# Low halves of weight blocks moved from GpSimd to VectorE, a beginning by halves of two blocks, and the closing norm's subtraction shared with GpSimd

## The chip, the cores and the metric

The kernel runs on one core of one Trainium2 chip. Its engines are TensorE (PE, products), VectorE (DVE), ScalarE (ACT), GpSimd (POOL) and SyncE (SP, which here only issues transfers). Each runs its own list of instructions in a fixed order, and they wait for each other through semaphores. The metric is the device time of one execution in microseconds (us); lower is better, and the verdict compares medians of runs.

## What is computed

A sequence of 512 positions of width 1024 passes through a macaron of layers, each with norms around it and, from the second half on, scales and shifts that a conditioning vector gives:

```
x = x + 0.5 * norm(swiglu(norm(x), w_gu, w_down))      # f1: width 2816
x = x + norm(hybrid_mixer(norm(x)))                    # gated recurrence and windowed attention
x = x + 0.5 * norm(swiglu(norm(x), w_gu, w_down))      # f2
x = layer_norm(x); retention; feed-forward (f3); neighbourhood attention; feed-forward (f4)
x = layer_norm(x)                                      # the closing norm

def rms_norm(x, g):
    y = x * lax.rsqrt(jnp.mean(x * x, axis=-1, keepdims=True) + RMS_EPS)
    return y * g

def swiglu(x, w_gu, w_down):
    gate, up = jnp.split(x @ w_gu, 2, axis=-1)
    return (jax.nn.silu(gate) * up) @ w_down
```

Everything is in float32.

## The kernel before, in words

**Products.** The activations lie as 8 chunks of 128 features by 512 positions, features on the partitions. A float32 product is made of three products of halves: a number is split into a high half (rounded to a shorter format) and a low half (what is left), and `products` issues three matmuls at L2072 (high weight, low activation), L2073 (low weight, high activation) and L2074 (high by high). Matmuls have 512 columns, or 256 where the positions are taken in two passes s = 0 and s = 1, as at the beginning and in the down products.

**A weight block.** Weights come in blocks of 128x1024 (512 KB; 128x768 for some of the first down product). SP loads a block into one of three raw buffers (the ring d_ring0 to 2), ScalarE casts it to the high half (L2394), and VectorE (L2764) or GpSimd (L3445) subtracts to get the low half; then the raw buffer is free for the next load. Which of the two does it is decided when the program is planned: by turns, except that VectorE does all of them for the down products of the third and fourth feed-forward ("dn3", "dn4") and where other chains of work are open. The first two blocks are cast and subtracted in halves of 512 columns (L2386, L2755).

**A swiglu unit.** For each 128 hidden features: gate and up products on TensorE; VectorE multiplies the gate by the norm's root (L3039); ScalarE takes silu (L2505); GpSimd multiplies by the root and the silu (L3451, the gate); VectorE multiplies by the up product in PSUM (L3052); ScalarE casts the result to its high half (L2514); VectorE subtracts for the low half (L3058, into `t_hid`). The down product waits for that last step of the last unit.

**A norm's root.** ScalarE squares the chunks, VectorE adds them up (L2881) and makes the last sum at L2887; TensorE sums over the partitions (L2208); ScalarE takes the root (L2440), VectorE the reciprocal (L2940) and a diagonal (L2944); TensorE turns it into a row (L2216). The second pass of the first norm goes this way at 17 to 39 us.

**Order.** A planner simulates the engines with a table of costs (a cast so long, a load so long) and lists each engine's steps by their due times; the program then holds these fixed lists. Every step keeps its place whatever happens on the chip.

**The closing norm's end.** For the second pass (256 positions) the variance's root is made as above while VectorE takes the mean row from each of the 8 chunks (`lead_z`, L2934, which reads the row from PSUM); when the root's row stands in PSUM, VectorE multiplies (`ln_apply`, L2993), ScalarE adds the shift and SP stores.

Of the kernel before, what the change touches and what calls it, by code (L numbers as in the profile page):

```python
# [40 lines left out]
SPARED = ()  # L41
# [142 lines left out]
class Plan(dict):  # L184
# [24 lines left out]
    def note(self, name, out, a, k):  # L209
# [118 lines left out]
    def run(self, families):  # L328
# [8 lines left out]
        while events:  # L337
# [3 lines left out]
            for engine in self.ops:  # L341
                while free[engine] <= t:
# [18 lines left out]
                    if op.table is not None and op.table != table:  # L361
# [34 lines left out]
def schedule(known=()):  # L396
# [124 lines left out]
    def assign(slot, after):  # L521
# [71 lines left out]
    def one_by_one(specs, segs):  # L593

        held = [block(sp[0], sp[1]) for sp in specs]
        for si, (t0, n) in enumerate(segs):
            force_tokens(t0, n)
            groups = []
            for (_, _, nk, src, outs), j in zip(specs, held):
                ready(j)  # L600
                b = bank()
                groups.append(put("mm", w=j, slot=where[j], lo=low[j], base=0, nk=nk, src=src, t0=t0, n=n, bank=b, po=0,
                                  before=seat(b, outs[0][1], len(items))))
# [192 lines left out]
    def last_norm(j, ready):  # L796
# [27 lines left out]
        for c in range(DC):  # L824
# [832 lines left out]
    first_ffn("f1", 1, "gu1", "dn1", "ffn1_post_g", lambda j, s: ("d_x1" if s else f"d_x0{j // 4}", 0),  # L1657
# [40 lines left out]
    for it in items:  # L1698
        if it.kind in ("ada", "load") or it.kind == "prep" and not it.q:
# [14 lines left out]
        if it.kind == "prep_lo":  # L1714
            it.update(preps[it.j], kind="prep_lo")
# [253 lines left out]
def sync_program(e, w, S, m, dram, items, loads):  # L1969
# [33 lines left out]
    def serve(it):  # L2003
        if it.kind == "setup":
            x_all, x_in = m.X[:, :].rearrange("p (c t) -> p c t", c=DC), dram["x"].rearrange("c p t -> p c t")
            e.dma_start(m.PAR[:, :], dram["params"]).then_inc(*S["d_par"].of(0))
            for half in range(2):
                some = slice(half * 4, half * 4 + 4)
                e.dma_start(x_all[:, some, 0:256], x_in[:, some, 0:256]).then_inc(*S[f"d_x0{half}"].of(0))
                part_of_block(0, half)  # L2010
            loaded[0] = len(HALVED)
            for r in HALVED[1:]:
                for half in range(2):
                    part_of_block(r, half)
            ring(NR)
            e.dma_start(m.CON[:, :], dram["consts"]).then_inc(*S["d_con"].of(0))
        elif it.kind == "x_load":
            x_all, x_in = m.X[:, :].rearrange("p (c t) -> p c t", c=DC), dram["x"].rearrange("c p t -> p c t")
            e.dma_start(x_all[:, :, 256:512], x_in[:, :, 256:512]).then_inc(*S["d_x1"].of(0))
# [50 lines left out]
def tensor_program(e, w, S, m, items):  # L2070
# [38 lines left out]
    def mm(it):  # L2109
        out = m.PS[:, it.bank, 0:it.n]  # L2110
        for k in range(it.nk):
            if k:
                yield
            xhi, xlo = moving(it, k)
            if k == 0:
                w.wait_ge(it.lo, (it.w, 0) if it.w in HALVED else it.w)
# [5 lines left out]
        done.then_inc(*S["ps"].of(it.id))  # L2122
# [242 lines left out]
def scalar_program(e, w, S, m, items):  # L2365
# [12 lines left out]
    def prep(it):  # L2378
        j = it.j
        if j in HALVED:  # L2380
            for half in range(2):
                some = slice(half * 512, half * 512 + 512)
                if half:
                    yield
                w.wait_ge(f"d_half{j}{half}", 0)
                e.copy(m.WHI[:, it.slot, some], m.RAW[:, j, some]).then_inc(*S["hi"].of((j, half), j))  # L2386
# [327 lines left out]
    def na_y(it):  # L2714
# [3 lines left out]
        for hd in range(2):  # L2718
# [8 lines left out]
            "att_scores": att_scores, "att_turn": att_turn, "att_sq": att_sq, "lru_sq": lru_sq, "root_sqrt": root_sqrt, "lead_sq": lead_sq, "lead_shift": lead_shift, "lead_sqrt": lead_sqrt,  # L2727
# [8 lines left out]
def vector_program(e, w, S, m, items):  # L2736
# [10 lines left out]
    def prep_lo(it):  # L2747
        j = it.j
        if j in HALVED:
            for half in range(2):  # L2750
                some = slice(half * 512, half * 512 + 512)
                if half:
                    yield
                w.wait_ge("hi", (j, half))
                e.tensor_tensor(m.WLO[:, it.slot, some], m.RAW[:, j, some], m.WHI[:, it.slot, some], ALU.subtract).then_inc(  # L2755
                    *S["lo_dve"].of((j, half), j))
# [171 lines left out]
    def lead_z(it):  # L2928
# [4 lines left out]
        w.wait_ge("x_mid", ("l11", it.c, 1))  # L2933
        e.tensor_tensor(x, x, m.PS[:, it.bank, 0:256], ALU.subtract).then_inc(*S["x_mid"].of(("l11z", it.c)))  # L2934
# [498 lines left out]
def gpsimd_program(e, w, S, m, items):  # L3433
# [24 lines left out]

    def na_setup(it):
# [3 lines left out]
    def na_bias(it):  # L3463
        w.wait_ge("d_misc", "mask2")
        for hd in range(2):
# [8 lines left out]
            "ret_copy": ret_copy, "na_setup": na_setup, "na_bias": na_bias}  # L3474
# [161 lines left out]
```

## Time and profile before

| | |
|---|---|
| median of 3 runs | 2797.17 us (2794.99 to 2798.91) |
| the profiled execution: its own time | 2799.06 us |
| the profiled execution: its span | 2797.2 us, mean granted TensorE clock 0.998 |
| busy: TensorE, VectorE, ScalarE, GpSimd | 2766.6, 1893.6, 1237.3, 402.0 us |

The span runs from the first to the last instruction that the profiler saw; the execution's own time is 1.9 us longer. An engine is busy while an instruction of it runs; matmuls overlap, so a busy TensorE is not one at its peak.

### The profile page before, as it was taken

What the parts mean: (1) busy time and instruction counts of PE and PEld (TensorE: products, weight loads), DVE (VectorE), ACT (ScalarE), POOL (GpSimd) and SP (SyncE); (2) the same over time, 40 slices, a digit from 0 to 9 for tenths busy, and PEclk for the clock granted to TensorE, in tenths of its full rate; (3) what the DMA queues carried; (4) which work ended last, traced back from release to release, by engine and by line L of the source; (5) the groups of instructions that cost most, each with busy time, mean ns of one, the idle gap of its engine ahead of it and who ended that gap; (6) DMA issues with size and microseconds to landing.
All of it is one profiled execution on the core that took longest, in us unless ns stands there. A gap on an engine that the chain in (4) does not pass through costs nothing.

```text
span 2797.2 us, 42563 instructions
## 1 busy us (share of the span) xinstructions
PE 2766.6 (99%) x16554; PEld 2459.0 (88%) x16554; DVE 1893.6 (68%) x3430; ACT 1237.3 (44%) x2248; POOL 402.0 (14%) x219
## 2 busy tenths in 40 slices
PE   9999999999999999999999999999999999999998
PEld 8888896988888888888888999999997787989898
DVE  7788788858895653444435896666686636778686
ACT  5332358642233552332314653344355546545353
POOL 2243300023332011011011000000001323000000
PEclk9999999999999999999999999999999999999999
DMA  6565512236554211111011112222223121222322
GB/s 204 184 189 188 166 64 83 84 104 221 188 191 134 77 54 61 38 61 61 31 61 50 43 54 82 61 68 72 72 76 102 50 76 54 75 83 91 106 91 83
DMA packets 86024, 267.91 MB, mean 96 GB/s; under 512 B 9152, under 2 KB 18752, under 8 KB 85568
## 3 DMA queue, kind: packets, MB, share of 16 engines
q1 hardware_dynamic: 85824, 265.20, 29.6%
q8 instruction: 131, 2.15, 0.3%
q14 instruction: 69, 0.57, 0.1%
HBM read 261.49 MB, written 2.10 MB: 94 GB/s over the span
## 4 chain that ended last, share of the span: by engine, by line
PE 87%; DVE 7%; DMA 3%; ACT 2%; issue 2%; SPq 0%; DVEq 0%; ACTq 0%
PE ps L2072 27%; PE ps L2073 27%; PE ps L2074 27%; DMA t_raw<-in_gu 2%; DVE t_wlo L2764 2%; PE ps L2351 1%; PE ps L2335 1%; PE ps L2324 1%; ACT t_whi L2394 1%; DMA t_x<-in_x 0%; PE ps L2216 0%; DMA t_raw<-in_dn 0%; PE ps L2208 0%; DVE t_raw L2773 0%; PE ps L2267 0%
## 5 line engine op out<-in xcount | busy, mean ns | idle before, releaser
L2072 PE MATMUL ps<-t_h,t_whi 128*128 128x512 f32 (+2 forms) x2152 | 727.3, 338 | 5.0 <-DVE t_wlo L2755 1.9
L2073 PE MATMUL ps<-t_h,t_wlo 128*128 128x512 f32 (+2 forms) x2152 | 721.3, 335 | 0.0
L2074 PE MATMUL ps<-t_h,t_whi 128*128 128x512 f32 (+2 forms) x2152 | 721.1, 335 | 0.0
L2394 ACT CAST t_whi<-t_raw 128x1024 fp32r<-128x1024 f32 (+3 forms) x449 | 368.4, 830 | 565.7 <-PE ps L2074 369.4
L2072 PEld LDWEIGHTS ps<-t_h,t_whi 128*128 128x128 f32 x2152 | 408.3, 190 | 50.3 <-issue 9.9
L2073 PEld LDWEIGHTS ps<-t_h,t_wlo 128*128 128x128 f32 x2152 | 408.5, 190 | 36.5 <-issue 1.2
L2074 PEld LDWEIGHTS ps<-t_h,t_whi 128*128 128x128 f32 x2152 | 408.3, 190 | 35.4
L2072 PE MATMUL ps<-t_hid,t_whi 128*128 128x256 f32 (+2 forms) x1320 | 428.4, 325 | 1.9 <-DVE t_hid L3058 1.7
L2073 PE MATMUL ps<-t_hid,t_wlo 128*128 128x256 f32 (+2 forms) x1320 | 426.1, 323 | 0.0
L2074 PE MATMUL ps<-t_hid,t_whi 128*128 128x256 f32 (+2 forms) x1320 | 425.5, 322 | 0.0
L2764 DVE TENSOR_TENSOR t_wlo<-t_raw,t_whi 128x512 fp32r<-128x512 f32 (+3 forms) x360 | 321.4, 902 | 106.9 <-ACT t_whi L2394 104.0
L3445 POOL TENSOR_TENSOR t_wlo<-t_raw,t_whi 128x1024 fp32r<-128x1024 f32 (+1 forms) x89 | 220.0, 2472 | 902.6 <-ACT t_whi L2394 902.6
L3010 DVE CUSTOM_DVE_ANT_0 t_m<-t_raw,t_m 128x1024 f32<-128x1024 f32 x192 | 296.4, 1580 | 49.5 <-DMA t_raw<-in_ada 40.8
L2072 PEld LDWEIGHTS ps<-t_hid,t_whi 128*128 128x128 f32 x1320 | 251.8, 191 | 22.5 <-DVE t_hid L3058 2.3
L2074 PEld LDWEIGHTS ps<-t_hid,t_whi 128*128 128x128 f32 x1320 | 251.6, 191 | 18.6
L2073 PEld LDWEIGHTS ps<-t_hid,t_wlo 128*128 128x128 f32 x1320 | 251.7, 191 | 18.3
L3445 POOL TENSOR_TENSOR t_xw<-t_raw,t_xw 128x1024 fp32r<-128x1024 f32 (+1 forms) x8 | 21.9, 2739 | 728.5 <-DVE t_x L3079 518.1
L2072 PE MATMUL ps<-t_mw,t_whi 128*128 128x256 f32 (+1 forms) x394 | 121.4, 308 | 1.4 <-ACT t_tmp L2399 1.4
L2074 PE MATMUL ps<-t_mw,t_whi 128*128 128x256 f32 (+1 forms) x394 | 121.2, 308 | 0.0
L2073 PE MATMUL ps<-t_mw,t_wlo 128*128 128x256 f32 (+1 forms) x394 | 121.2, 308 | 0.0
L3079 DVE SCALAR_TENSOR_TENSOR t_m<-ps,t_mod,t_m 128x512 f32<-128x512 f32 (+1 forms) x79 | 51.2, 648 | 85.1 <-PE ps L2074 84.8
L2072 PE MATMUL ps<-t_wlo,t_h 128*128 128x512 f32 x264 | 103.8, 393 | 0.0
(355 smaller groups left out, 4840.6 us busy)
## 6 DMA issues: line engine op xcount, KB each, us to landing
t_raw<-in_gu SPq DMA_DIRECT2D x174, 512.0 KB, 3.4
t_raw<-in_ada SPq DMA_DIRECT2D x96, 512.0 KB, 3.6
t_raw<-in_dn SPq DMA_DIRECT2D x52, 512.0 KB, 4.2
t_raw<-in_dn SPq DMA_DIRECT2D x24, 384.0 KB, 3.4
t_raw<-in_ret_v SPq DMA_DIRECT2D x16, 512.0 KB, 3.5
t_raw<-in_ret_qk SPq DMA_DIRECT2D x16, 512.0 KB, 3.3
t_raw<-in_ret_g SPq DMA_DIRECT2D x16, 512.0 KB, 3.4
t_raw<-in_ret_o SPq DMA_DIRECT2D x16, 512.0 KB, 3.8
```

What stands on the lines that cost most here:

```text
L2072: e.matmul(out, whi, xlo, start=first, stop=False, skip_group_check=shared)
L2073: e.matmul(out, wlo, xhi, start=False, stop=False, skip_group_check=shared)
L2074: return e.matmul(out, whi, xhi, start=False, stop=last, skip_group_check=shared)
L2324: done = e.matmul(m.PS[:, hd, :].rearrange("p (a t) -> p a t", a=2), m.na_q(qpart, it.c, it.b * P, P)[pp], m.na_keys(kpart, it.c, BAND0[it ...
L2335: done = e.transpose(m.PS[:, 2 + hd, kt * P:(kt + 1) * P], s[:, kt * P:(kt + 1) * P], m.ident)
L2351: done = e.matmul(m.PS[hd * 64:hd * 64 + 64, 4 + hd, it.b * P:(it.b + 1) * P], m.at(v, 64), m.na_t(it.to[hd])[:, kt // 2, kt % 2 * P:(kt % ...
L2394: e.copy(m.block(0, it.slot, n), m.raw(it)).then_inc(*S["hi"].of(j))
L2764: e.tensor_tensor(m.block(1, it.slot, n), m.raw(it), m.block(0, it.slot, n), ALU.subtract).then_inc(*S["lo_dve"].of(j))
L3010: e.tensor_tensor_reduce(m.at(ADA_OUT + who * 1024, 1024), m.RAW[:, it.raw % NR, :], m.cond(who), 1.0, 0.0, ALU.mult, ALU.add, m.mod(it.la ...
L3079: e.scalar_tensor_tensor(out=out, in0=ps, scalar=m.mod(it.layer, it.who, it.gm, it.j), in1=old, op0=ALU.mult, op1=ALU.add).then_inc(*S["dr ...
L3445: e.tensor_tensor(m.block(1, it.slot, n), m.raw(it), m.block(0, it.slot, n), ALU.subtract).then_inc(*S["lo_pool"].of(j))
```

## The change

1. Low halves: VectorE does those of the first ten blocks (`EARLY`) and of the down products "dn1" and "dn2" as well. In all 25 low halves leave GpSimd's list (109 before, 84 after) and stand on VectorE's.
2. The beginning: SP loads the first halves of the first two blocks ahead of the second halves, and TensorE multiplies the first four chunks with both blocks' first halves before it turns to the second halves. The second pass's x comes in two loads instead of one. The first pass's root moves back in ScalarE's and TensorE's lists, behind the second pass's scaled x.
3. The closing norm: ScalarE copies the mean row from PSUM (`lead_copy`), GpSimd subtracts it from chunks 7, 6 and 5, and VectorE from the other five; only one of these now stands ahead of the reciprocal.
4. The planner's cost of a load: its time now follows its size, after a latency of 2000 (ns), where each load counted alike before. The lists of all engines are ordered anew by it; beside the beginning they differ most in the mixer (about 430 to 490 us).

```
-SPARED = ()
+EARLY = 10
+SPARED = (5, 6, 7)
...
-            takes, lasts = 480, 3300
+            takes, lasts, table = 480, 1270 * n / 1024, 2000
...
-                        landed = max(t + lasts, landed + 1270)
+                        landed = max(t + op.table, landed) + lasts
...
-        if chains or state["begin"] or state["held"] is not None or j < len(known) and known[j][0][0] in ("dn3", "dn4"):
+        if j in HALVED:
+            low[j] = "lo_dve"
+            if j == HALVED[-1]:
+                for half in range(2):
+                    for i in HALVED:
+                        put("prep", j=i, slot=where[i], after=after, lo="lo_dve", q="", half=half)
+                        put("prep_lo", j=i, half=half)
+            return
+        if j < EARLY or chains or state["begin"] or state["held"] is not None or j < len(known) and known[j][0][0] in ("dn1", "dn2", "dn3", "dn4"):
             low[j] = "lo_dve"
...
-        for c in range(DC):
+        put("lead_copy", bank=row)
+        for c in (*SPARED[::-1], *range(SPARED[0])):
             put("lead_z", c=c, bank=row, pool=c in SPARED)
...
             for half in range(2):
                 some = slice(half * 4, half * 4 + 4)
                 e.dma_start(x_all[:, some, 0:256], x_in[:, some, 0:256]).then_inc(*S[f"d_x0{half}"].of(0))
-                part_of_block(0, half)
+                for r in HALVED:
+                    part_of_block(r, half)
...
+        if it.c:
+            w.wait_ge("root_dve", ("diag", "l11v", 1))
+        w.wait_ge("lead_copy", 0)
         e.tensor_tensor(x, x, m.PS[:, it.bank, 0:256], ALU.subtract).then_inc(*S["x_mid"].of(("l11z", it.c)))
...
+    def lead_z(it):
+        if it.pool:
+            x = m.x(it.c, 256, 256, "l11")
+            w.wait_ge("lead_copy", 0)
+            w.wait_ge("root_dve", ("diag", "l11v", 1))
+            w.wait_ge("x_mid", ("l11", it.c, 1))
+            e.tensor_tensor(x, x, m.acc(1, 3), ALU.subtract).then_inc(*S["x_pool"].of(("l11z", it.c)))
```

**GpSimd's list at the beginning.** Before: two gates, two low halves of weight blocks (t_wlo), two gates of the second pass, the low half of another block.

```order
7 L3451 TENSOR_TENSOR t_m<-t_m,t_tmp 128x256 [waits silu,d_par]
8 L3451 TENSOR_TENSOR t_m<-t_m,t_tmp 128x256 [waits silu]
9 L3445 TENSOR_TENSOR t_wlo<-t_raw,t_whi 128x1024 [waits hi,d_ring1]
10 L3445 TENSOR_TENSOR t_wlo<-t_raw,t_whi 128x1024 [waits hi,d_ring0]
11 L3451 TENSOR_TENSOR t_m<-t_m,t_tmp 128x256 [waits silu] x2
12 L3445 TENSOR_TENSOR t_h<-t_raw,t_h 128x4x256 [waits hi,d_ring2]
```

Now (lines are 21 further down):

```order
7 L3472 TENSOR_TENSOR t_m<-t_m,t_tmp 128x256 [waits silu,d_par]
8 L3472 TENSOR_TENSOR t_m<-t_m,t_tmp 128x256 [waits silu]
9 L3466 TENSOR_TENSOR t_wlo<-t_raw,t_whi 128x1024 [waits hi,d_ring1]
10 L3472 TENSOR_TENSOR t_m<-t_m,t_tmp 128x256 [waits silu] x2
11 L3472 TENSOR_TENSOR t_m<-t_m,t_tmp 128x512 [waits silu] x4
12 L3466 TENSOR_TENSOR t_xw<-t_raw,t_xw 128x4x256 [waits hi,d_ring1]
```

Two of the three early low halves are gone, and the one that is left is that of a block after the tenth; on VectorE's list the low halves of the third to the tenth block stand between the norms' adds instead.

**VectorE's list at the end of f2's last swiglu part.** Before: the last gate products (L3039), one low half (L2764), the two last units' up products (L3052) and low halves of hidden features (L3058), one low half between.

```order
1075 L3039 TENSOR_TENSOR t_m<-ps,t_tmp 128x512 [waits drain_dve,ps]
1076 L3010 ISA t_m,t_mod<-t_raw,t_m 128x1024 [waits ada]
1077 L3010 ISA t_mod 128x1
1078 L3058 TENSOR_TENSOR t_hid<-t_tmp,t_hid 128x512 [waits hid_hi]
1079 L3039 TENSOR_TENSOR t_m<-ps,t_tmp 128x512 [waits drain_dve,ps]
1080 L2764 TENSOR_TENSOR t_wlo<-t_raw,t_whi 128x1024 [waits hi,d_ring1]
1081 L3052 TENSOR_TENSOR t_tmp<-t_m,ps 128x512 [waits hid_lo,gate_pool,ps]
1082 L3058 TENSOR_TENSOR t_hid<-t_tmp,t_hid 128x512 [waits hid_hi]
1083 L3052 TENSOR_TENSOR t_tmp<-t_m,ps 128x512 [waits hid_lo,gate_pool,ps]
1084 L2764 TENSOR_TENSOR t_wlo<-t_raw,t_whi 128x1024 [waits hi,d_ring0]
1085 L3058 TENSOR_TENSOR t_hid<-t_tmp,t_hid 128x512 [waits hid_hi]
```

Now (L2764 is L2782, L3010 L3031, and L3039, L3052 and L3058 are L3060, L3073 and L3079):

```order
1104 L3031 ISA t_m,t_mod<-t_raw,t_m 128x1024 [waits ada]
1105 L3031 ISA t_mod 128x1
1106 L3060 TENSOR_TENSOR t_m<-ps,t_tmp 128x512 [waits drain_dve,ps]
1107 L2782 TENSOR_TENSOR t_wlo<-t_raw,t_whi 128x1024 [waits hi,d_ring0]
1108 L3060 TENSOR_TENSOR t_m<-ps,t_tmp 128x512 [waits drain_dve,ps]
1109 L2782 TENSOR_TENSOR t_wlo<-t_raw,t_whi 128x1024 [waits hi,d_ring1]
1110 L3073 TENSOR_TENSOR t_tmp<-t_m,ps 128x512 [waits hid_lo,gate_pool,ps]
1111 L2782 TENSOR_TENSOR t_wlo<-t_raw,t_whi 128x1024 [waits hi,d_ring2]
1112 L3079 TENSOR_TENSOR t_hid<-t_tmp,t_hid 128x512 [waits hid_hi]
1113 L3073 TENSOR_TENSOR t_tmp<-t_m,ps 128x512 [waits hid_lo,gate_pool,ps]
1114 L2782 TENSOR_TENSOR t_wlo<-t_raw,t_whi 128x1024 [waits hi,d_ring0]
1115 L3079 TENSOR_TENSOR t_hid<-t_tmp,t_hid 128x512 [waits hid_hi]
```

Four low halves stand among these steps where two did; the two added ones were on GpSimd, one ahead of the last two gates and one behind them.

**VectorE's list in the closing norm.** Before: the first subtraction of the mean (L2934), the variance (L2925), two subtractions, the reciprocal (L2940), the diagonal (L2944), and three more after two and five products (L2993).

```order
3116 L2934 TENSOR_TENSOR t_m<-t_m,ps 128x256 [waits ps]
3117 L2925 SCALAR_TENSOR_TENSOR t_st<-ps,t_tmp 128x2 [waits lead_shift,ps]
3118 L2934 TENSOR_TENSOR t_m<-t_m,ps 128x256 x2
3119 L2940 RECIPROCAL t_st<-t_st 128x2 [waits root_act]
3120 L2944 TENSOR_SCALAR t_tmp<-t_con,t_st 128x128 [waits root_dve,hid_lo]
3121 L2944 TENSOR_SCALAR t_tmp<-t_con,t_st 128x128
3122 L2934 TENSOR_TENSOR t_m<-t_m,ps 128x256 x2
3123 L2993 SCALAR_TENSOR_TENSOR t_m<-t_m,t_par,ps 128x256 [waits ps,x_mid]
3124 L2993 SCALAR_TENSOR_TENSOR t_m<-t_m,t_par,ps 128x256 [waits x_mid] x4
3125 L2934 TENSOR_TENSOR t_m<-t_m,ps 128x256 x2
3126 L2993 SCALAR_TENSOR_TENSOR t_m<-t_m,t_par,ps 128x256 [waits x_mid] x2
3127 L2934 TENSOR_TENSOR t_m<-t_m,ps 128x256
```

Now (L2934 is L2955, L2925 L2943, L2940 L2961, L2944 L2965, L2993 L3014):

```order
3140 L2943 SCALAR_TENSOR_TENSOR t_st<-ps,t_tmp 128x2 [waits lead_shift,ps]
3141 L2955 TENSOR_TENSOR t_m<-t_m,ps 128x256 [waits lead_copy]
3142 L2961 RECIPROCAL t_st<-t_st 128x2 [waits root_act]
3143 L2965 TENSOR_SCALAR t_tmp<-t_con,t_st 128x128 [waits root_dve,hid_lo]
3144 L2965 TENSOR_SCALAR t_tmp<-t_con,t_st 128x128
3145 L2955 TENSOR_TENSOR t_m<-t_m,ps 128x256 [waits root_dve]
3146 L2955 TENSOR_TENSOR t_m<-t_m,ps 128x256
3147 L3014 SCALAR_TENSOR_TENSOR t_m<-t_m,t_par,ps 128x256 [waits ps,x_mid]
3148 L3014 SCALAR_TENSOR_TENSOR t_m<-t_m,t_par,ps 128x256 [waits x_mid] x2
3149 L2955 TENSOR_TENSOR t_m<-t_m,ps 128x256 x2
3150 L3014 SCALAR_TENSOR_TENSOR t_m<-t_m,t_par,ps 128x256 [waits x_mid] x2
3151 L3014 SCALAR_TENSOR_TENSOR t_m<-t_m,t_par,ps 128x256 [waits x_pool]
```

One subtraction instead of three stands ahead of the reciprocal, and two instead of three come after the first product; three wait on GpSimd (x_pool).

## Rows read from the trace of the kernel before

**Rows 1.** The page: busy time of each engine, share of the span, instructions.

```profile
PE 2766.6 (99%) x16554; PEld 2459.0 (88%) x16554; DVE 1893.6 (68%) x3430; ACT 1237.3 (44%) x2248; POOL 402.0 (14%) x219
```

**Rows 2.** Timeline of TensorE: start, us, instruction, idle before and its releaser.

```profile
8.18 0.36 PE L2072 MATMUL ps<-t_h,t_whi 128*128 128x256 f32 x1 [0.92 <-DVE t_wlo L2755]
...
33.03 0.73 PE L2208 MATMUL ps<-t_con,t_m 128*128 128x128 f32 x4 [1.91 <-DVE t_m L2887]
...
457.85 0.47 PE L2072 MATMUL ps<-t_h,t_whi 128*128 128x512 f32 x1 [1.14 <-DVE t_m L3136]
...
872.62 0.39 PE L2072 MATMUL ps<-t_hid,t_whi 128*128 128x256 f32 x1 [1.72 <-DVE t_hid L3058]
```

**Rows 3.** Windows: PE, PEld, DVE, ACT, POOL busy, granted clock, DMA share, GB/s.

```profile
33.00:37.00 4.00, 3.97 (x21) 3.98 (x22) 2.33 (x6) 2.48 (x3) 1.87 (x1) 0.57 0.79 242
873.00:877.00 4.00, 4.00 (x24) 4.00 (x23) 0.42 (x1) 0.42 (x1) 0.00 (x0) 0.57 0.48 134
...
457.00:461.00 4.00, 3.15 (x14) 2.63 (x15) 3.93 (x15) 4.00 (x14) 0.00 (x0) 1.00 0.00 0
```

**Rows 4.** Timeline of TensorE behind the wait at 33 us.

```profile
36.33 0.41 PE L2073 MATMUL ps<-t_h,t_wlo 128*128 128x256 f32 x1
36.54 0.41 PE L2074 MATMUL ps<-t_h,t_whi 128*128 128x256 f32 x1
...
37.23 0.28 PE L2072 MATMUL ps<-t_h,t_whi 128*128 128x256 f32 x1
37.35 0.28 PE L2073 MATMUL ps<-t_h,t_wlo 128*128 128x256 f32 x1
```

**Rows 5.** Timeline of VectorE and GpSimd at 15 to 33 us.

```profile
15.40 0.42 DVE L2887 TENSOR_TENSOR t_m<-t_m 128x256 f32<-128x256 f32 x1
...
29.25 1.22 DVE L2764 TENSOR_TENSOR t_xw<-t_raw,t_xw 128x1024 fp32r<-128x1024 f32 x1
...
29.73 2.96 POOL L3445 TENSOR_TENSOR t_wlo<-t_raw,t_whi 128x1024 fp32r<-128x1024 f32 x1 [2.11 <-ACT t_whi L2394]
30.39 2.58 DVE L2887 TENSOR_TENSOR t_m<-t_m 128x256 f32<-128x256 f32 x1
```

**Rows 6.** Timeline of GpSimd and VectorE at the end of f2's last swiglu part.

```profile
850.49 1.29 POOL L3451 TENSOR_TENSOR t_m<-t_m,t_tmp 128x512 f32<-128x512 f32 x1
...
863.77 3.55 POOL L3451 TENSOR_TENSOR t_m<-t_m,t_tmp 128x512 f32<-128x512 f32 x2
867.29 2.39 POOL L3445 TENSOR_TENSOR t_wlo<-t_raw,t_whi 128x1024 fp32r<-128x1024 f32 x1
...
863.70 1.23 DVE L2764 TENSOR_TENSOR t_wlo<-t_raw,t_whi 128x1024 fp32r<-128x1024 f32 x1 [1.56 <-ACT t_whi L2394]
...
867.54 2.69 DVE L3058 TENSOR_TENSOR t_hid<-t_tmp,t_hid 128x512 fp32r<-128x512 f32 x1 [0.69 <-ACT t_hid L2514]
870.15 0.68 DVE L3052 TENSOR_TENSOR t_tmp<-t_m,ps 128x512 f32<-128x512 f32 x1
...
871.89 0.68 DVE L3058 TENSOR_TENSOR t_hid<-t_tmp,t_hid 128x512 fp32r<-128x512 f32 x1
```

**Rows 7.** Timeline of ScalarE at the beginning.

```profile
5.09 1.71 ACT L2460 ACTIVATE t_h<-t_x,t_par 128x256 fp32r<-128x256 f32 x4 [1.91 <-DMA t_x<-in_x]
```

**Rows 8.** Timeline of VectorE and ScalarE in the closing norm.

```profile
2787.93 0.74 DVE L2934 TENSOR_TENSOR t_m<-t_m,ps 128x256 f32<-128x256 f32 x2
2788.05 0.20 ACT L2455 ACTIVATE t_st<-t_st 128x2 f32<-128x2 f32 x1 [0.90 <-DVE t_st L2925]
2788.59 0.16 DVE L2940 RECIPROCAL t_st<-t_st 128x2 f32<-128x2 f32 x1
```

**Rows 9.** Groups of GpSimd's instructions: count, busy, mean ns, idle before.

```profile
L3445 POOL TENSOR_TENSOR t_wlo<-t_raw,t_whi 128x1024 fp32r<-128x1024 f32 (+1 forms) x89 | 220.0, 2472 | 902.6 <-ACT t_whi L2394 902.6
...
L3470 POOL TENSOR_TENSOR t_m<-t_m 128x256 f32<-128x256 f32 x48 | 43.5, 927 | 71.6 <-DVE t_m L3389 65.8 <-DMA t_m<-in_rpb 5.5
```

**Rows 10.** Windows of f2, columns as in rows 3.

```profile
800.00:840.00 40.00, 40.00 (x178) 33.10 (x178) 37.81 (x48) 10.94 (x14) 15.70 (x7) 1.00 0.59 195
```

More of the change, by code:

```diff
@@ L597, in one_by_one @@
             force_tokens(t0, n)
-            groups = []
+            groups, begun = [], {}
+            if si == 0:
+                for (_, _, nk, src, outs), j in zip(specs, HALVED):
+                    begun[j] = bank()
+                    put("mm", w=j, slot=where[j], lo=low[j], base=0, nk=nk, ks=(0, 1, 2, 3), src=src, t0=t0, n=n, bank=begun[j], po=0,
+                        before=[])
             for (_, _, nk, src, outs), j in zip(specs, held):
                 ready(j)
-                b = bank()
+                b = begun[j] if j in begun else bank()
                 groups.append(put("mm", w=j, slot=where[j], lo=low[j], base=0, nk=nk, src=src, t0=t0, n=n, bank=b, po=0,
-                                  before=seat(b, outs[0][1], len(items))))
+                                  before=seat(b, outs[0][1], len(items)), ks=range(4 if j in begun else 0, nk)))
                 tick(nk * (n + 32) / 800)
@@ L1698, in schedule @@
     for it in items:
-        if it.kind in ("ada", "load") or it.kind == "prep" and not it.q:
+        if it.kind == "prep" and it.get("half") == 1:
+            it["raw"] = it.j
+        elif it.kind in ("ada", "load") or it.kind == "prep" and not it.q:
             it["raw"] = len(loads)
@@ L1714, in schedule @@
         if it.kind == "prep_lo":
-            it.update(preps[it.j], kind="prep_lo")
+            it.update({**preps[it.j], "kind": "prep_lo", "half": it.get("half")})
     return items, loads
@@ L2018, in serve @@
             x_all, x_in = m.X[:, :].rearrange("p (c t) -> p c t", c=DC), dram["x"].rearrange("c p t -> p c t")
-            e.dma_start(x_all[:, :, 256:512], x_in[:, :, 256:512]).then_inc(*S["d_x1"].of(0))
+            for half in range(2):
+                some = slice(half * 4, half * 4 + 4)
+                e.dma_start(x_all[:, some, 256:512], x_in[:, some, 256:512]).then_inc(*S[f"d_x1{half}"].of(0))
         elif it.kind in ("prep", "ada", "load"):
@@ L2110, in mm @@
         out = m.PS[:, it.bank, 0:it.n]
-        for k in range(it.nk):
-            if k:
+        ks = it.get("ks", range(it.nk))
+        for k in ks:
+            if k != ks[0]:
                 yield
             xhi, xlo = moving(it, k)
-            if k == 0:
-                w.wait_ge(it.lo, (it.w, 0) if it.w in HALVED else it.w)
+            if k == ks[0]:
+                w.wait_ge(it.lo, (it.w, k // 4) if it.w in HALVED else it.w)
                 wait_all(it.before)
@@ L2380, in prep @@
         if j in HALVED:
[L2381 to L2386, printed above, removed]
+            some = slice(it.half * 512, it.half * 512 + 512)
+            w.wait_ge(f"d_half{j}{it.half}", 0)
+            e.copy(m.WHI[:, it.slot, some], m.RAW[:, j, some]).then_inc(*S["hi"].of((j, it.half), j))
             return
@@ L2450, in lead_shift, with lead_copy @@
             *S["lead_shift"].of(0))
+    def lead_copy(it):
+        w.wait_ge("ps", "lead_mean")
+        w.wait_ge("ps", "lead_row")
+        e.copy(m.acc(1, 3), m.PS[:, it.bank, 0:256]).then_inc(*S["lead_copy"].of(0))
     def lead_sqrt(it):
@@ L2749, in prep_lo @@
         if j in HALVED:
[L2750 to L2756, printed above, removed]
+            some = slice(it.half * 512, it.half * 512 + 512)
+            w.wait_ge("hi", (j, it.half))
+            e.tensor_tensor(m.WLO[:, it.slot, some], m.RAW[:, j, some], m.WHI[:, it.slot, some], ALU.subtract).then_inc(
+                *S["lo_dve"].of((j, it.half), j))
         elif it.lo == "lo_dve":
```

16 lines of the change are left out of this document (7 added, 9 removed).

## The prediction

> **What bounds the kernel now.** I read the page first: TensorE is busy 2766.6 us of the 2797.2 [rows 1], so only the thirty microseconds in which it stands still, and any time in which it runs slowly, are to be had. Next its timeline, picking out the rows that carry an idle time. The list is short, and two entries stand out because the change touches what released them: 1.91 us at 33.03, ended by VectorE's sum L2887, and 1.72 us at 872.62, ended by its L3058 [rows 2]. Then the windows behind these two. The granted clock over 33 to 37 and over 873 to 877 is 0.57; behind the 1.14 us wait at 457.85 it is 1.00 [rows 2, 3]. So each of the two longer waits has a tail in which TensorE works at the lower of its two levels (1.2 instead of 2.4 GHz). At the two levels alone, a mean of 0.57 over 4 us is 3.44 us at the lower one ((1 - 0.57) / 0.5 x 4). Matmuls start every 0.21 us in the tail and every 0.12 us after it [rows 4], so a tail costs 3.44 x (1 - 0.12 / 0.21) = 1.5 us. Last, the timelines of the releasers. L2887 takes 0.42 us at 15.40 but 2.58 at 30.39, and it ends 0.28 us behind a low half that GpSimd began at 29.73 [rows 5]. L3058 takes 0.68 at 871.89 but 2.69 at 867.54, beside GpSimd's low half of 867.29 to 869.68 [rows 6]. A VectorE instruction that reads two operands from SBUF waits here for the whole of GpSimd's.
>
> **The change part by part.** Low halves first. One costs GpSimd 2.47 us [rows 9] and VectorE 1.22 [rows 5]; 25 of them take some 62 us from GpSimd, which costs nothing by itself, and put 30.5 us on VectorE, which has 903 us idle over the span [rows 1]. What matters is where.
>
> *At 33 us.* GpSimd's low half ahead of the second pass's gates is no longer there in the changed list, and VectorE's own low half ahead of the sum was there before. At its short length the sum would have ended at 30.39 + 0.42 = 30.81. TensorE came free at 33.03 - 1.91 = 31.12 [rows 2, 5]. So the wait goes, with a margin of 0.3 us, and its tail with it: 1.9 + 1.5 = 3.4 us. Bounds: in the changed list ScalarE does the second pass's scaling of x earlier than the first pass's root, which helps the sum, while VectorE has more low halves in its first 30 us. If two of these stand in the way (2.4 us, less the margin) the wait is 2.1 and nothing is won: 0 to 3.4. I take 3.4, since only one stands directly ahead of the sum, as before.
>
> *At 872 us.* Without the lock the first of the two L3058 is 2.0 us shorter, and with it everything behind it: the last one would start at 869.9 and end at 870.6, before TensorE comes free at 872.62 - 1.72 = 870.9 [rows 2, 6]. Two low halves of 1.22 come in. One stands ahead of the first up product, where VectorE was waiting for the gate. The other fills the time in which ScalarE casts (0.69 idle ahead of 867.54), and overhangs it by some 0.5. So the last L3058 ends at about 871.1, and a wait of 0.2 is left, too short for a tail: 1.7 - 0.2 + 1.5 = 3.0 us. Were both low halves wholly in the way, it would end at 873.0 and all be as before: 0 to 3.2. The same place in f1 showed no wait and has more cover, since 512-column products stand ahead of the down product's narrow ones there; I count nothing for it.
>
> *The beginning.* The first product waits 0.92 us for the first low half [rows 2]. ScalarE scaled four chunks before it cast, at 0.43 us each [rows 7]; two of these now go behind the cast. That is worth 0.86 if the half block has landed by then and nothing if it has not. I take 0.4. The later waits of the first groups, on second halves instead of on the second block, I set as equal.
>
> *The closing norm.* The reciprocal begins at 2788.59, behind two subtractions, though its root was there at 2788.25 [rows 8]: 0.34 earlier. Of the subtractions behind the first product, two are left of three, at 0.37: together 0.7 us, nothing if the added copy of the row holds the root up. GpSimd's three take 0.93 each in the nearest rows [rows 9], 2.8 us from the diagonal on. They are first needed behind TensorE's product with the diagonal and seven instructions of VectorE of about 0.4 each [rows 5, 8]: hidden, with the product's time to spare. If not, up to 0.7 is lost again.
>
> *The planner's reordering.* In the mixer all lists move. The waits there are single ones of about 1 us, such as 457.85 [rows 2]. I take nothing; bounds of -2 to +2 us, since one wait of that size may go or come, with a tail where it grows.
>
> **Sum:** 3.4 + 3.0 + 0.4 + 0.7 = 7.5 us. From the profiled execution, span 2797.2 and own time 2799.06, that gives a span of 2789.7 and 2791.6. That execution is 1.9 above the median of the runs, 2797.17, so for the median I say 2797.2 - 7.5 = 2789.7.
>
> **A rule against it.** GpSimd's two gates of 863.77 took 3.55 us where one takes 1.29 at 850.49, so the pair lost 1.0; VectorE's low half of 863.70 ran beside their beginning [rows 6]. The lock works both ways. The Trainium skill ("SBUF — State Buffer", section "SBUF: two separate sides") says that VectorE and GpSimd share a pair of ports which whichever instruction starts first holds to its end, for a VectorE instruction with two SBUF inputs against one of GpSimd that reads SBUF. By that rule, which the trace bears out in both directions here, each low half that moves can hold up a gate instead of being held up by one.
>
> **Rivals.**
> *(a) The lock turned round.* A low half of 1.22 in front of each of the last two gates makes each 1.0 later, the up product waits for the gate, and the last L3058 ends 2 us later than I say: the wait at 872 comes back with its tail. For it speaks the pair at 863.77; against it, that GpSimd is then free of its own 2.9 us low half ahead of the gates. Gain 7.5 - 3.0 = 4.5: 2792.7. The same holds if instead the sum at 33 us is late (gain 4.1: 2793.1).
> *(b) No net change.* Both waits come back, or one does while the mixer's new order makes a wait with a tail (1.7 + 1.5 = 3.2): gain 0 to 1.5, about 2796.5. Before and after differ in so many list places that this can't be excluded from the rows.
> *(c) Slower: VectorE becomes the bound in f2.* From 800 to 840 VectorE is busy 37.8 us of 40 [rows 10], 2.2 idle, with four GpSimd low halves in it. If these moved without relieving it of locks it would need 37.8 + 4 x 1.22 = 42.7, and TensorE would wait 2.7 and pay a tail, 4.2 us in each such stretch. f1 has like stretches. Three of them give 12.6 - 7.5 = 5 slower, 2802; the point from which it decides is two. Against it: a lock costs VectorE 2 us [rows 5, 6], more than the 1.22 it takes over, so where the low half used to collide VectorE gains.
>
> **How the numbers follow.** The forecast, 0.55; (a) in either form, 0.22; (b), 0.13; (c), 0.10. 0.2% is 5.6 us, about what a measurement of this kernel tells from no change. The forecast's own range, with the end and the beginning at their bounds and the mixer at -2 to +2, is 2786.5 to 2792.5. Only what gains over 5.6, below 2791.6, counts as faster: nearly all of the forecast and a little of (a), 0.55 in all. Same: the rest of (a) and of the forecast, (b), and a part of (c), 0.36. Slower: 0.09. For eight in ten the range goes from 2786.5 to 2797, leaving out most of (c) and a few gains beyond the bounds.
>
> **What would show it.** In the changed kernel's profile: no idle row above 0.5 us at the sum over the second pass (about 30 us), nor at the first narrow down product of f2 (about 866), with the granted clock at 1.00 behind both; the sum L2905 at 0.42 us and L3079 at 0.68, with no GpSimd low half beside them; the first product at 7.8 instead of 8.18; the reciprocal 0.3 us behind the root's row rather than 0.5, and the end of the last product not waiting for GpSimd. The prediction is wrong if one of the two waits stands there under another releaser, if a gate on GpSimd of over 2 us ends late ahead of the last up product, or if TensorE shows new waits of over 1.5 us between 400 and 510 or in 800 to 840.

## The result and the profile after

The changed kernel is **slower**, by little: median 2799.82 us against 2795.03 over 22 runs each, ratio 1.0018 with a 95% interval of 1.0012 to 1.0024. Forecast were 2789.7 and a gain of 0.27%; the time moved the other way, by 4.8 us, which is clear of the interval though under the 0.2% that the prediction drew as its line for "same". Two more things stand in the times. The 22 runs of before lie between 2793.3 and 2798.9; the execution whose profile the forecast used, 2799.06, lay above them all. And the runs of the changed kernel spread from 2795.3 to 2807.8, over twice as far. Its profiled execution took 2798.53 us.

The page's busy times first, as in [rows 1]:

```profile
PE 2764.7 (99%) x16554; PEld 2456.8 (88%) x16554; DVE 1906.1 (68%) x3452; ACT 1236.8 (44%) x2251; POOL 340.9 (12%) x197
```

GpSimd lost 61 us, and VectorE took only 12.5 more, not the forecast's 30.5: summed over the two traces, its low halves of weight blocks take 33.5 more, but the low halves of hidden features (L3058, now L3079), for one, take 12.8 less. Then TensorE's timeline, the rows with an idle time that answer to [rows 2], and the largest of those that are new or longer (f4 has some more, of 0.4 to 0.7):

```profile
7.80 0.36 PE L2089 MATMUL ps<-t_h,t_whi 128*128 128x256 f32 x1 [0.51 <-DVE t_wlo L2773]
26.32 0.71 PE L2235 MATMUL ps<-t_tmp,t_con 128*128 128x128 f32 x4 [0.71 <-DVE t_tmp L2965]
31.57 0.60 PE L2227 MATMUL ps<-t_con,t_m 128*128 128x128 f32 x3 [0.23 <-DVE t_m L2905]
...
455.25 0.47 PE L2089 MATMUL ps<-t_h,t_whi 128*128 128x512 f32 x1 [1.91 <-DVE t_m L3157]
523.57 0.39 PE L2089 MATMUL ps<-t_hid,t_h 128*128 128x256 f32 x1 [0.84 <-POOL t_h L3466]
740.07 0.50 PE L2089 MATMUL ps<-t_hid,t_whi 128*128 128x512 f32 x1 [0.81 <-DVE t_hid L3079]
869.34 0.38 PE L2089 MATMUL ps<-t_hid,t_whi 128*128 128x256 f32 x1 [0.62 <-DVE t_hid L3079]
985.94 0.38 PE L2089 MATMUL ps<-t_hid,t_mw 128*128 128x256 f32 x1 [0.64 <-DVE t_hid L3354]
1551.11 0.70 PE L2190 MATMUL ps<-t_m,t_con 128*128 128x256 f32 x2 [0.81 <-DVE t_m L2905]
```

Both waits that the forecast wanted gone are short here, 0.23 and 0.62. New are 0.71 at the first pass's root row, 0.84 at 523, 0.81 at 740 and at 1551, and the mixer's wait has grown from 1.14 to 1.91, a wait of over 1.5 between 400 and 510, which the prediction had named as a sign of being wrong. The row at 985 stands for four, one in each retention head. The windows behind the old places and the mixer's wait, columns as in [rows 3]:

```profile
31.00:35.00 4.00, 3.77 (x32) 3.57 (x32) 3.96 (x8) 3.97 (x6) 1.10 (x2) 1.00 0.56 172
455.30:459.30 4.00, 4.00 (x22) 3.41 (x23) 3.90 (x11) 3.98 (x12) 0.00 (x0) 1.00 0.00 0
869.00:873.00 4.00, 3.66 (x30) 3.67 (x31) 0.83 (x3) 0.42 (x1) 0.00 (x0) 1.00 0.46 135
```

No tail stands behind any of these. Set beside the first profile by the start of the same matmuls, TensorE is 2.7 us ahead at 39 us, 2.6 at 455, 2.0 at 742, 4.7 at 877 (the wait and the tail of [rows 2, 3] are missed there), but 2.7 at 1551 and 0.15 at 2741, behind waits that no term of the sum named. VectorE at the second pass's sum, and its reciprocal, answer to [rows 5, 8]; below them stand ScalarE's root and SP's last stores:

```profile
30.55 0.97 DVE L2905 TENSOR_TENSOR t_m<-t_m 128x256 f32<-128x256 f32 x1
...
2787.91 0.20 ACT L2476 ACTIVATE t_st<-t_st 128x2 f32<-128x2 f32 x1 [0.27 <-DVE t_st L2943]
2788.14 0.17 DVE L2961 RECIPROCAL t_st<-t_st 128x2 f32<-128x2 f32 x1
...
2789.03 2.09 POOL L3486 TENSOR_TENSOR t_m<-t_m 128x256 f32<-128x256 f32 x3 [328.93 <-DVE t_tmp L2965]
2790.83 4.12 SPq L2080 DMA_DIRECT2D out_x<-t_m  x8
```

The sum takes 0.97, beside two gates and not a low half. The reciprocal follows the root's start by 0.23 instead of 0.54. GpSimd's subtractions end 0.5 us before VectorE's second group of products begins.

### The profile page after: what moved, and what is told of

Its sections match the earlier page's. It is cut to its first block and busy times, and to the rows that moved or that the text cites. A ratio compares the mean times of both kernels' runs of the same rounds, so it can differ in the third digit from the quotient of the medians.

```text
span 2796.7 us, 42566 instructions
## 1 busy us (share of the span) xinstructions
PE 2764.7 (99%) x16554; PEld 2456.8 (88%) x16554; DVE 1906.1 (68%) x3452; ACT 1236.8 (44%) x2251; POOL 340.9 (12%) x197
## 3 DMA queue, kind: packets, MB, share of 16 engines
q8 instruction: 131, 2.15, 0.3%
## 5 line engine op out<-in xcount | busy, mean ns | idle before, releaser
L2782 DVE TENSOR_TENSOR t_wlo<-t_raw,t_whi 128x512 fp32r<-128x512 f32 (+3 forms) x379 | 343.8, 917 | 107.8 <-ACT t_whi L2410 104.7
L3031 DVE CUSTOM_DVE_ANT_0 t_m<-t_raw,t_m 128x1024 f32<-128x1024 f32 x192 | 301.0, 1599 | 42.8 <-DMA t_raw<-in_ada 38.8
L3466 POOL TENSOR_TENSOR t_wlo<-t_raw,t_whi 128x1024 fp32r<-128x1024 f32 x70 | 180.2, 2574 | 778.1 <-ACT t_whi L2410 778.1
L2090 PE MATMUL ps<-t_whi,t_h 128*128 128x512 f32 x264 | 102.8, 390 | 0.0
```

The source lines that it names most:

```text
L2090: e.matmul(out, wlo, xhi, start=False, stop=False, skip_group_check=shared)
L2782: e.tensor_tensor(m.block(1, it.slot, n), m.raw(it), m.block(0, it.slot, n), ALU.subtract).then_inc(*S["lo_dve"].of(j))
L3031: e.tensor_tensor_reduce(m.at(ADA_OUT + who * 1024, 1024), m.RAW[:, it.raw % NR, :], m.cond(who), 1.0, 0.0, ALU.mult, ALU.add, m.mod(it.la ...
L3466: e.tensor_tensor(m.block(1, it.slot, n), m.raw(it), m.block(0, it.slot, n), ALU.subtract).then_inc(*S["lo_pool"].of(j))
```

## The experiments

Ratios are to the kernel before, run beside each experiment on the same chip, with the 95% interval behind them; where a range in microseconds follows, it is the lowest and the highest run. The four parts of the change are named: *lows* (the first ten blocks and dn1, dn2 on VectorE), *start*, *end*, *cost* (of a load).

**Before and after once more** (no edit).

> The kernel before, unchanged, for a second profile and a spread. Theory A (the two waits at 33 and 872 us are there in every execution): span near 2797 again, both idle rows of 1.7 to 1.9 us with a tail at a granted clock of 0.57 behind each. Theory B (they depend on the execution, and the first profile caught a bad one, 4 us over the median of 22 runs): one of the two is shorter or has no tail, span near 2793. Ratio 1.000 by both.

> The changed kernel, unchanged, for a second profile and a spread: its 22 runs went from 2795 to 2808 us. Theory A (a VectorE step that waits for a load of in_ada stands ahead of an L3079 that TensorE needs, at 740 us in the first profile, and the load's landing varies): in this profile the idle row at 740 differs from the 0.81 us of the first by as much as the load landed sooner or later, and where it goes over 1.7 us a tail follows. Theory B (the spread comes from the mixer's wait at 455 us, 1.91 without a tail in the first profile, with a tail in others): the row at 740 stays at 0.8, the one at 455 stays at 1.9 and shows a tail in a slow execution. Ratio 1.0018 by both, spread over 8 us.

Measured: before 1.0002 (0.9994 to 1.0011), own time of the profiled execution 2794.74, span 2792.9. In it the two places read, on TensorE's timeline and in windows behind them:

```profile
32.81 0.71 PE L2208 MATMUL ps<-t_con,t_m 128*128 128x128 f32 x4 [1.74 <-DVE t_m L2887]
37.41 0.71 PE L2216 MATMUL ps<-t_tmp,t_con 128*128 128x128 f32 x4 [1.02 <-DVE t_tmp L2944]
870.65 0.39 PE L2072 MATMUL ps<-t_hid,t_whi 128*128 128x256 f32 x1 [0.62 <-DVE t_hid L3058]
```

```profile
33.00:37.00 4.00, 3.39 (x28) 3.19 (x27) 3.96 (x6) 2.49 (x3) 2.10 (x1) 1.00 0.75 239
870.00:874.00 4.00, 3.38 (x29) 3.35 (x29) 1.02 (x2) 0.42 (x1) 0.00 (x0) 1.00 0.54 170
```

Theory B holds: an execution near the median has neither tail, and at 872 us a wait of 0.62, which is what the changed kernel has. Some 4 us of what the forecast wanted to win are absent here: they come and go by execution (x9, below, has them in part). After: 1.0036 (1.0023 to 1.0050), 2798.5 to 2805.9 in five runs; in its profile the row at 740 is absent and the mixer's wait, 1.94, has a tail (granted clock 0.61 over 454.6 to 458.6). Both waits vary, then, but this profile is of the fastest of the five, so it doesn't show what makes the slow ones.

**The lows alone, the cost alone.**

```
-        if chains or state["begin"] ... known[j][0][0] in ("dn3", "dn4"):
+        if j < 10 or chains or state["begin"] ... known[j][0][0] in ("dn1", "dn2", "dn3", "dn4"):
```

> The kernel before with its low halves of the first ten blocks and of dn1 and dn2 on VectorE, nothing else. Its lists differ from before's in f2 and the retention, not in the mixer or f4. Theory A (the low halves bring the waits on in_ada loads and the spread): ratio 1.000 to 1.003, a spread of 8 us or more, the wait at 872 shortened to under 0.7, a new one at about 742, and the four retention heads at 0.64 instead of 0.36. Theory B (the new cost of a load is to blame, the low halves do what was forecast): ratio 0.997 to 0.999, spread as before's, 6 us.

The cost alone takes the three lines of the change's diff in the planner.

> The kernel before with the planner's new cost of a load, nothing else. Its lists differ from before's at the start, in the mixer and in f4. Theory A (the low halves are to blame): ratio 1.000 to 1.001, spread as before's; f4 loses about 2 us to longer waits, 0.07%. Theory B (the new cost is to blame): ratio 1.002 or more, spread of 8 us or more, the mixer's wait at 455 to 458 us at 1.9 or above.

Measured: lows alone 1.0037 (1.0023 to 1.0050), 2797.6 to 2809.3 in five runs; cost alone 1.0018 (1.0009 to 1.0027), 2796.6 to 2803.5, the mixer's wait 1.94 with a tail. Each is slower by itself: the lows by more than was expected, the cost by a little less than its theory B asked for, and without the wide spread. x3's profile shows the worst of its waits, VectorE's and SP's timelines ahead of it:

```profile
737.73 1.60 DVE L2764 TENSOR_TENSOR t_wlo<-t_raw,t_whi 128x1024 fp32r<-128x1024 f32 x1
...
743.99 1.23 DVE L3010 CUSTOM_DVE_ANT_0 t_m<-t_raw,t_m 128x1024 f32<-128x1024 f32 x1 [3.46 <-DMA t_raw<-in_ada]
745.14 0.69 DVE L3058 TENSOR_TENSOR t_hid<-t_tmp,t_hid 128x512 fp32r<-128x512 f32 x1
```

```profile
739.40 0.33 SPq L1993 DMA_DIRECT2D t_raw<-in_ada  x1
```

```profile
745.88 0.52 PE L2072 MATMUL ps<-t_hid,t_whi 128*128 128x512 f32 x1 [4.31 <-DVE t_hid L3058]
```

A weight block's low half on VectorE ends at 739.33 and, by the times, frees its raw buffer; SP issues the load of a conditioning block (in_ada) at 739.40; it is there at 743.99; and VectorE's step on it (L3010) stands in front of the L3058 that TensorE needs. TensorE waits 4.31 us and has a tail behind it (granted clock 0.57 over 745.9 to 749.9).

**Parts taken out, and that step put behind.** x5 and x9 keep only start and end; x6 is the changed kernel with the old cost. In x7 (on x3) and x8 (on the changed kernel) VectorE's list is changed after planning:

```
+        v = order["vector"]
+        for i in range(len(v)):
+            j = i
+            while v[j][0].kind == "up_lo" and j and v[j - 1][0].kind == "ada":
+                v[j - 1], v[j] = v[j], v[j - 1]
+                j -= 1
```

> The kernel before with the beginning by halves and the shared closing norm only; low halves by turns and the old cost of a load, so that the lists of all engines are as before from 60 us to the closing norm. If these two edits do what was forecast (0.4 at the first product, the waits for the second pass's sum or root shortened by one to two, 0.7 at the end): 2.5 to 4 us faster than before, ratio 0.9986 to 0.9991. If they bring nothing or their waits move to the root row: 0.9996 to 1.0002.

> The kernel of x5_start_and_end_only once more, for a profile of an ordinary execution (the first one's ran over 7 ms). Theory A (the beginning by halves only moves waits: GpSimd's low half still stands beside the second pass's sum): up to the first 512-column product at about 39 us nothing is won, the closing norm is 0.35 us shorter, ratio 0.9996 to 1.0006. Theory B (first result was noise): 1 to 2 us won by 39 us, ratio 0.9990 to 0.9995.

> The changed kernel with the planner's old cost of a load. Theory A (the low halves make VectorE wait for in_ada loads ahead of the last L3079 of a part of f2, the new cost makes the mixer's wait 1.9 us with a tail and lengthens f4's): the mixer's row is 1.15 again without a tail, f4 from its first products to the closing norm 288 us instead of 290.7, and the wait near 740 stays, between 0.8 and 4.3 by execution: ratio 1.000 to 1.003, spread over 7 us. Theory B (the new cost is the whole of the loss): ratio 0.998, spread 5 us.

> As x3_lows_only, but wherever one of VectorE's steps on in_ada blocks stands directly ahead of a low half of hidden features (L3058) in its list, the two are exchanged; nothing else. Theory A (that step holds up L3058 until a load lands): the 4.3 us wait and the tail at 746 us are gone, the one of 1.0 at 335 too, ratio from 1.0037 to 1.000 to 1.001, spread under 6 us. Theory B (VectorE is simply too late there with the low halves added): the wait stays within 1 us of what it was and the ratio at 1.003 or above.

> The changed kernel with the same exchange of VectorE's in_ada steps and the low halves of hidden features directly behind them. Theory A: no idle row above 0.7 near 740 us in any execution, ratio from 1.0018 to 1.0036 down to 1.0005 to 1.0015 (the mixer's wait with its tail, the retention's and f4's longer waits stay), spread under 6 us. Theory B: ratio and spread as the changed kernel's.

Measured: x5 1.0006 (0.9997 to 1.0015) and x9 1.0003 (0.9994 to 1.0012): start and end alone bring nothing that can be told. (One of x5's 11 executions, the profiled one, took 7056 us; it is left out, and its profile with it.) In x9 TensorE still waits 2.12 us for the second pass's sum, with a tail (granted clock 0.57 over 33 to 37); GpSimd's low half is still there. And at the end of f2, where its lists are those of before, the wait of the first profile is back, without a tail (1.00 over 872 to 876):

```profile
871.84 0.38 PE L2089 MATMUL ps<-t_hid,t_whi 128*128 128x256 f32 x1 [1.67 <-DVE t_hid L3079]
```

x6: 1.0021 (1.0009 to 1.0032), the mixer's wait back at 1.15, the row at 742 3.15 with a tail, 2794.1 to 2810.8. x7: 1.0034 (1.0021 to 1.0046), 2801.1 to 2805.7; x8: 1.0022 (1.0012 to 1.0032), 2797.7 to 2802.9. So the step on in_ada makes the wait at 742 us and most of the spread, since both are gone, but it does not make the median. In x7 3.96 us are waited at 338 instead:

```profile
330.70 1.23 DVE L2770 TENSOR_TENSOR t_wlo<-t_raw,t_whi 128x1024 fp32r<-128x1024 f32 x1 [2.97 <-ACT t_whi L2400]
```

Here, some 7 us earlier, VectorE waits for a down block's cast, and that (at 329.55, after 2.88 us) for its load; the steps that TensorE needs stand behind it in the list. Theory A as stated fell: one wait went and the next took its place.

**All that stands in front of L3079.** x11 (on the changed kernel) and x12 (with the old cost) exchange weight blocks' low halves too: `in ("ada", "prep_lo")` instead of `== "ada"`.

> The changed kernel, where each low half of hidden features (L3079) is put ahead of in_ada steps and of weight blocks' low halves that stand directly in front of it in VectorE's list. Theory A (what stands in front of L3079 at the end of a swiglu part and waits for a load is what costs, in whatever form): no idle row above 0.7 at 334, 740 and 869 us, spread under 5 us, ratio 1.0005 to 1.0012, the mixer's, retention's and f4's waits left. Theory B (VectorE's added work itself is too much in f1 and f2): rows of 1 us or more at two of the three places, ratio above 1.0018.

> As x11_hid_first, with the planner's old cost of a load. Theory A: the mixer's wait back to 1.15 without a tail and f4 2 us shorter as well, so only the retention's and the added 0.8 waits at 524 and 1553 us are left against the gains of the start and the end: ratio 0.9990 to 1.0000. Theory B: 1.0010 or above.

Measured: 1.0008 (0.9999 to 1.0016) and 1.0025 (1.0016 to 1.0033). x11 looks better than the changed kernel, though the intervals overlap, and its profile has 2.15 with a tail at 870; x12 has 2.81 at 337 and 2.03 at 624. Where the waits fall changes with the list, and this did not settle it.

**The turns.** What the diff does not say: blocks that go to VectorE by rule do not count in the turns. Behind an odd number of blocks left out of the count, every later block that goes by turns changes engine, all through the program. Of the first ten, three had taken turns before. So in the two kernels' plans, all 109 low halves that GpSimd had before are on VectorE now, and 84 others are on GpSimd: the 25 of the change's description are only the difference.

x10 has start and end, the first ten on VectorE, the old cost, and counts every block:

```
             turn["low"] = turn.get("low", 0) + 1
-            low[j] = ("lo_dve", "lo_pool")[turn["low"] % 2]
+            low[j] = ("lo_dve", "lo_pool")[turn["low"] % 2] if j >= EARLY else "lo_dve"
```

> The kernel before with the beginning by halves, the shared closing norm and the low halves of the first ten blocks on VectorE; those of dn1 and dn2 by turns as before, the turns counted as before, the old cost of a load. From 60 us to the closing norm all lists are as before's. If the gain at the start needs GpSimd's low half out of the way of the second pass's sum: 2.5 us won by the first 512-column product and 0.35 at the end, nothing lost behind, spread 6 us as before's: ratio 0.9987 to 0.9993. If even so nothing is won: 0.9998 to 1.0005.

Measured: **0.9989** (0.9980 to 0.9998), 2788.2 to 2792.5: faster than the kernel before. At 60 us TensorE is 3.6 us ahead of x9 and 3.5 of x1 (by the start of the same matmuls). Then one thing added to it at a time: x13 dn1's and dn2's lows, counted; x14 the new cost; x15 only `turn.get("low", 1)`, which exchanges the engines of the blocks by turns.

> x10_first_ten_on_vector plus the low halves of dn1's and dn2's blocks on VectorE, with the turns counted as if they had taken theirs, so that every other block's low half stays on its engine: lists differ from x10's in f1 and f2 only, the retention and f4 as before. Theory A (VectorE's list waits for the down blocks' loads in front of the last L3079 of a part): a wait of 1 to 4 us at one or more of 334, 620, 740, 870 us, another one by execution, spread over 7 us, ratio 1.000 to 1.002 against x10's 0.9989. Theory C (the loss came from the shifted turns, which change which blocks GpSimd takes everywhere): ratio 0.998 to 0.999, as x10.

> x10_first_ten_on_vector plus the planner's new cost of a load. Theory A (the cost is worth 1.4 to 1.8 us of time lost in the mixer with its tail, and up to 2 in f4): the mixer's row at 1.9 instead of 1.14, ratio 1.0000 to 1.0008. Theory C: ratio 0.9989, as x10.

> x10_first_ten_on_vector with the turns begun on the other engine, so that each of GpSimd's and VectorE's low halves by turns changes places, as many on each as before but one. Theory C (the shifted turns cost): the rows of 0.64 at the four retention heads, 0.84 at 524 and 0.81 at 1551 us are there, 2.7 us, ratio 0.9997 to 1.0005. Theory A (they cost next to nothing): ratio 0.9987 to 0.9993.

Measured: x13 0.9992 (0.9983 to 1.0000), x14 0.9997 (0.9988 to 1.0006), x15 **1.0026** (1.0017 to 1.0035). Under the old cost the down blocks' low halves cost nothing that can be told; shifting the turns costs 0.37%, 10 us by the ratios and 8.4 by the medians, over twice what x10 gains and far more than was expected of it. x15 exchanges the down blocks of f1 and f2 too, which the changed kernel has all on VectorE. The closer pair is x6 against x13: all down blocks on VectorE and the old cost in both, only the count differs. That is 1.0021 against 0.9992, 8 us. In their profiles x6 loses to x13 1.1 us at 524, 4.8 at 742 (its wait of 3.15 and the tail), 1.2 at the four retention heads and 0.8 at 1551.

The first retention head shows how, in x13 and in x15, VectorE and GpSimd of each:

```profile
978.84 2.42 POOL L3466 TENSOR_TENSOR t_wlo<-t_raw,t_whi 128x1024 fp32r<-128x1024 f32 x1 [3.35 <-ACT t_whi L2410]
983.72 1.02 DVE L3354 TENSOR_TENSOR t_hid<-t_m,t_hid 128x512 fp32r<-128x512 f32 x2
```

```profile
987.74 2.41 POOL L3466 TENSOR_TENSOR t_wlo<-t_raw,t_whi 128x1024 fp32r<-128x1024 f32 x1 [3.36 <-ACT t_whi L2410]
989.03 2.00 DVE L3354 TENSOR_TENSOR t_hid<-t_m,t_hid 128x512 fp32r<-128x512 f32 x2 [0.24 <-ACT t_hid L2675]
```

The same two instructions of L3354 take 1.02 us where GpSimd's low half is over before, and 2.00 beside it. TensorE waits for them: 0.36 against 0.65 us, in each of four heads. In f1 and f2 x15 waits 1.27 at 82, 1.17 at 205 and 1.75 with a tail at 873 us, x13 at none of these over 0.62. These three are not shown to be the changed kernel's loss: its profile has none of those at 82 and 205, and waits of 1.7 near 870 stand in x9, x14 and x16 too, where the turns are kept. Last, the changed kernel itself with the turns counted for all:

> The changed kernel with all its four parts, where the blocks that go to VectorE still count in the turns, so that every other block's low half stays on the engine that it had before. If the shift of the turns is what cost (x15: 1.0026 against x10's 0.9989): the four retention heads at 0.36, no rows at 524 and 1551 us, none of over 1 us at 740; the mixer's 1.9 and f4's waits left, which the new cost of a load brings (x14: 0.9997): ratio 0.9995 to 1.0003. If the down blocks' low halves and the new cost only hurt together: 1.0010 or above.

Measured: 1.0013 (1.0004 to 1.0022), 2796.3 to 2802.3. The rows came out as expected (0.36 at the heads, none at 524, 740 and 1551), the ratio did not: at the end of f2 TensorE waits twice, with a tail (granted clock 0.61 over 869.5 to 873.5).

```profile
867.17 0.39 PE L2089 MATMUL ps<-t_hid,t_whi 128*128 128x256 f32 x1 [1.73 <-DVE t_hid L3079]
869.50 0.58 PE L2089 MATMUL ps<-t_hid,t_whi 128*128 128x256 f32 x1 [1.71 <-DVE t_hid L3079]
```

That is the second branch of the expectation: without the down blocks' low halves the new cost gives 0.9997 (x14), with them 1.0013. With start, end and lows always in:

| | old cost | new cost |
|---|---|---|
| turns counted for all | x13 0.9992, spread 4.5 us | x16 1.0013, 5.9 |
| turns shifted | x6 1.0021, 16.8 | changed kernel 1.0018, 12.5; x2 1.0036 |

The shift costs 0.3% under the old cost, the new cost 0.2% with the turns kept; with the down blocks on VectorE either alone is enough to lose the gain, and without both it is there. Under the new cost the shift's price is between 0.05%, which the intervals don't tell from nothing, and 0.2%. So the two do not add. Both act by rewriting the same lists, which may be why; that is not shown.

## Why the prediction was wrong

**The failed step is what the change was said to move.** The change part by part counted 25 low halves from GpSimd to VectorE and asked only where these stand; it gave the rest of the moves to "the planner's reordering", in the mixer, at nothing or 2 us either way. Both were too small.
- *The turns.* The exception to the turns shifts them: 109 low halves go to VectorE and 84 others to GpSimd. That alone costs 8 us under the old cost (x6 against x13).
- *The reordering.* The new cost is worth 2 to 6 us (x14 against x10, x16 against x13). 0.8 of it is the mixer's wait of 1.9, with a tail in some executions, and 1 to 3 are f4's. From its first product to the closing norm's first sum f4 takes 288.1 (x1) and 288.5 (x3) with the old cost against 289.4 (x4) and 290.7 (x2) with the new; 287.8 (x15) and 288.3 (x13) against 291.0 (x14). These all ran on one chip. On the one of x9 to x12 all are shorter, 285.3 to 286.3 with the old cost against 287.2 (x11), so f4 is compared within a chip.

Without both, the rest of the change is a gain (x13, 0.9992).

**The base.** The sum was made against an execution of 2799.06, set down as 1.9 above the median of three; by 22 it was 4.0 above. Of the terms at 33 and 872 us, both tails, and 1.1 of the wait at 872, are absent in x1; x9 has the tail at 33 and 1.67 at 872. A term that stands in some executions only should have counted for a part.

Point by point:
- *At 33 us*: mechanism right, and needed: without the first ten lows on VectorE nothing is won (x9), with them the wait is at most 0.23 (the changed kernel; x10 shows none). In x10 the sum of 3.4 came out, 3.5 us against x1 with the beginning's share, but from other parts: x1 has no tail there, and its waits of 1.74 at the sum and 1.02 at the root row went. In the changed kernel 2.6 were won by 41 us against the first profile and 2.2 against x1, since 0.7 comes back at the root row. The margin of 0.3 went to gates on GpSimd beside the sum (0.97 instead of 0.42): rival (a)'s lock, in small.
- *At 872 us*: mechanism right, size by execution. No low half of GpSimd stands beside L3079 now, and 0.62 is left in five of the six profiles with the down blocks on VectorE and the planner's own order (the changed kernel, x2, x3, x6, x13); 0.2 was forecast. In the sixth, x16, VectorE stands 2.68 us for a down block's cast (865.29) in front of L3079, and that cast 2.59 for its load (864.14), as in x7. With before's lists there it is 1.72 (the first), 0.62 (x1), 1.67 (x9) and 0.75 (x10), so the gain is nothing in one execution and 1.1 in the next. Elsewhere in f2 the wait of rival (a)'s kind came, by a way that it didn't name: a raw buffer freed later, a load issued later, and a step waiting for it in front of L3079 (x3).
- *The beginning*: the first product starts 0.38 earlier, 0.4 forecast, but the agreement is luck. With the new beginning it starts between 7.8 (x2) and 8.9 (x13), with the old one between 8.0 (x4) and 8.4 (x1, x3).
- *The closing norm*: the reciprocal 0.3 earlier as forecast, GpSimd's part hidden as forecast. But from the first sum to the end 0.35 were won and not 0.7. Counted from that sum ScalarE's last result is 0.73 earlier; SP, which issues the stores one after another, is by then behind it: its last issue starts at 2794.50, 0.27 after the result, and at before's end 0.03 after it.
- *Rival (c)*: not seen. VectorE is not the bound; x13 has 26 more low halves on it than before and is as fast as x10 within the intervals.
- *Rival (b)* was nearest, for its second reason: list places.

Why an execution waits 0.8 or 4.3 us at 740 was not followed further than to the landing of a load. Why x12 is slower than x11, and whether the load that x16 waits for is late in most of its executions, stays open.

## What to carry to other kernels

When an exception takes items out of an alternation, keep counting them, or the whole rest of the program can change engine; compare the lists of every engine over the whole program, not only where the edit acts. Where a step on a shared in-order queue frees a buffer, follow it on: buffer, load, next user, and what is queued behind that user. And take the base from several executions: a forecast that removes waits seen in one profile should know whether the next execution has them.

## What was unexpected of the hardware

A wait of about 1.9 us on TensorE is followed by a tail at the lower clock in some executions and not in others, with the same list: at 455 us 1.91 and a granted clock of 1.00 in the first profile after, 1.94 and 0.61 in the second.

A VectorE instruction that reads one tensor from SBUF was held up by GpSimd too. In x1 the diagonal's two tensor_scalar took 2.69 us beside a low half on GpSimd, and TensorE waited 1.02 for them at 37.41; in the changed kernel (34.77) they took 0.48 with none beside them:

```profile
34.90 2.37 POOL L3445 TENSOR_TENSOR t_wlo<-t_raw,t_whi 128x1024 fp32r<-128x1024 f32 x1 [2.43 <-ACT t_whi L2394]
34.67 2.69 DVE L2944 TENSOR_SCALAR t_tmp<-t_con,t_st 128x128 f32<-128x128 f32 x2
```

The Trainium skill ("SBUF — State Buffer", section "Who interferes with whom") has a case for it: a VectorE instruction in a two-port mode contends with GpSimd even with a single input. The row agrees with that; no run here shows which mode the instruction ran in.
